# Modulation sums as column-tiled matmuls, and indexer scores in head pairs between the steps of the keys' projection

## What is computed

```python
mod = jax.nn.silu(c) @ ada_w + ada_b            # c: 1 x 1024, ada_w: 1024 x 6144
sh1, sc1, g1, sh2, sc2, g2 = jnp.split(mod, 6, axis=-1)
h = rms_norm(x, norm1_g) * (1.0 + sc1[:, None, :]) + sh1[:, None, :]
proj = h @ w_in                                 # 1024 x 2888
rq, rk, rv, rg, aq, ak, av, iq, ik, iw = jnp.split(proj, ...)
# indexer, for each block of 128 queries
rel = jnp.einsum('bqhe,bse->bqhs', qib, k_idx)  # 8 heads of 64
score = jnp.einsum('bqhs,bqh->bqs', jax.nn.relu(rel), wb)
score = jnp.where(causal, score, -jnp.inf)
_, sel = lax.top_k(score, 128)
# retention, attention over sel, then
x = x + g1 * (mix @ w_o)
h2 = rms_norm(x, norm2_g) * (1.0 + sc2) + sh2
y = moe(h2, ...)                                # 32 experts, the top 4 of each token
return rms_norm(x + g2 * y, final_g)
```

## Time and profile before

| | us |
|---|---|
| median of 3 runs | 1601.48 |
| lowest, highest | 1601.24, 1601.77 |
| the profiled execution, its own time | 1605.01 |
| its span, first to last instruction | 1603.2 |
| PE busy in the span | 1489.5 (93%) |
| DVE busy | 1329.3 (83%) |
| ACT busy | 1085.5 (68%) |
| POOL busy | 422.0 (26%) |

### The profile page before, as it was taken

How to read it: one execution, slowest core, us unless ns; L and a number is a source line. 1 busy time by engine, 2 the same in 40 slices (tenths; PEclk the granted TensorE clock), 3 DMA queues, 4 the chain that set the end, 5 groups by cost and what they waited for, 6 DMA issues and landing times.

```text
span 1603.2 us, 20619 instructions
## 1 busy us (share of the span) xinstructions
PE 1489.5 (93%) x6872; PEld 1185.7 (74%) x6872; DVE 1329.3 (83%) x1153; ACT 1085.5 (68%) x1126; POOL 422.0 (26%) x341
## 2 busy tenths in 40 slices
PE   3999996896799999999999999999999999999993
PEld 3667963455588888888888888888888888888872
DVE  4689957366599999998999999998999999998992
ACT  3554325333677777788877777788877777788881
POOL 1113510101113322233223322233223423233221
PEclk8899987996899999999999999999999999999996
DMA  9745510225499999999999999999999999999974
GB/s 348 219 156 184 184 54 14 60 79 202 177 365 372 364 364 373 374 370 382 360 372 371 370 365 372 370 375 379 357 378 370 376 348 370 382 379 368 362 272 132
DMA packets 95983, 483.70 MB, mean 302 GB/s; under 512 B 23416, under 2 KB 32752, under 8 KB 43632
## 3 DMA queue, kind: packets, MB, share of 16 engines
q1 hardware_dynamic: 83200, 450.47, 72.2%
q0 software_dynamic: 12752, 32.84, 8.6%
HBM read 469.09 MB, written 23.61 MB: 307 GB/s over the span
## 4 chain that ended last, share of the span: by engine, by line
PE 83%; DVE 9%; ACT 3%; DMA 3%; issue 1%; SPq 0%; POOLq 0%; DVEq 0%; POOL 0%; ACTq 0%
PE bank L1364 15%; PE bank L1363 15%; PE bank L1365 15%; PE bank L1385 7%; PE bank L1387 7%; PE bank L1386 7%; PE bank L1246 3%; PE bank L1344 2%; PE bank L1356 2%; PE bank L1336 2%; DVE w_lo L1474 2%; DMA ring<-in_ada_w 1%; PE bank L1067 1%; PE bank L1068 1%; PE bank L1069 1%
## 5 line engine op out<-in xcount | busy, mean ns | idle before, releaser
L1513 DVE TENSOR_TENSOR e_lo<-ring,e_hi 128x2048 fp32r<-128x2048 f32 x384 | 868.4, 2289 | 93.9 <-ACT e_hi L742 93.4
L742 ACT ACTIVATE e_hi<-ring 128x2048 fp32r<-128x2048 f32 x384 | 728.5, 1914 | 235.8 <-PE bank L1365 234.6
L1363 PE MATMUL bank<-e_hi,x_hi 128*128 128x512 f32 x1024 | 405.9, 396 | 1.6 <-DVE e_lo L1513 1.6
L1364 PE MATMUL bank<-e_lo,x_hi 128*128 128x512 f32 x1024 | 402.5, 393 | 0.0
L1365 PE MATMUL bank<-e_hi,x_lo 128*128 128x512 f32 x1024 | 398.8, 389 | 0.0
L1363 PEld LDWEIGHTS bank<-e_hi,x_hi 128*128 128x128 f32 x1024 | 192.7, 188 | 48.4 <-DVE e_lo L1513 2.5
L1364 PEld LDWEIGHTS bank<-e_lo,x_hi 128*128 128x128 f32 x1024 | 193.1, 189 | 40.0
L1365 PEld LDWEIGHTS bank<-e_hi,x_lo 128*128 128x128 f32 x1024 | 192.8, 188 | 40.2
L1385 PE MATMUL bank<-e_hi,act_hi 128*128 128x512 f32 x512 | 208.5, 407 | 0.1
L1387 PE MATMUL bank<-e_hi,act_lo 128*128 128x512 f32 x512 | 201.9, 394 | 0.0
L1386 PE MATMUL bank<-e_lo,act_hi 128*128 128x512 f32 x512 | 201.1, 393 | 0.0
(11 more groups left out here) (247 smaller groups left out, 1800.4 us busy)
## 6 DMA issues: line engine op xcount, KB each, us to landing
ring<-in_w_gu SPq DMA_DIRECT2D x256, 1024.0 KB, 8.6
ring<-in_w_down SPq DMA_DIRECT2D x128, 1024.0 KB, 7.3
ring<-in_ada_w SPq DMA_DIRECT2D x24, 1024.0 KB, 7.3
ring<-in_w_in SPq DMA_DIRECT2D x9, 1024.0 KB, 5.9
ring<-in_w_o SPq DMA_DIRECT2D x4, 1024.0 KB, 7.6
ring<-in_w_in SPq DMA_DIRECT2D x10, 256.0 KB, 5.9
sum_rows<-xs POOLq DMA_DIRECT2D x5, 512.0 KB, 4.5
xs<-in_x SPq DMA_DIRECT2D x4, 512.0 KB, 4.9
```

The source lines that it names most:

```text
L742: return nc.scalar.activation(dst, src, ACT.Copy, scale=scale)
L1363: pe.matmul(bank[b][:], x_hi[:, c, :], hi, start=False, stop=False)
L1364: pe.matmul(bank[b][:], x_hi[:, c, :], lo, start=False, stop=False)
L1513: tt(e_lo[c % PARTS][:], raw(period.raw_slot(c)), e_hi[:, c % PARTS, :].bitcast(F32), ALU.subtract).then_inc(lo_ready, 1)
```

## The change

The partial sums on ACT, DVE and POOL are gone. A piece of `ada_w` now stays in its slot, and PE multiplies it as it is: `mod_rows` issues four float32 matmuls for it, each with 32 equal columns of silu(c) as weights and 512 columns of the piece as the moving part. The four write the partition groups 0, 32, 64 and 96 of one bank, and eight pieces add up there. The bank is copied to `mrow` (by DVE for A, by ACT for the two halves of B, `rows_out_of_bank`), turned by four transposes (for A in the opening, for B in `rest_turned`), and `modA` and `modB` are read out of the turned rows; the gate rows g1 and g2 are added to their bias on 64 partitions (`gate_rows`) and stored by four DMAs.

The B pieces are now in the order of the two halves of their columns, and each is multiplied by PE just ahead of the half of `w_in` that follows it in `SEQUENCE` (`rest_rows`): three ahead of half 6, one, two, one and two ahead of halves 8, 10, 12 and 14, one and two ahead of the two parts of rg, two and one ahead of the two parts of rv, one behind rv. PE frees their slots.

The scores have a count and four banks (3 to 6) of their own. They are issued in pairs of heads, and behind each of the first eight pairs stands one step (three matmuls) of half 6. In the opening, the low parts of halves 0 and 1 stand behind `a1` on DVE. All four `sigmoid_rg` stand ahead of the eight takes of rv on ACT.

```diff
+            def mod_rows(b, n, k, used):
+                have(n)
+                for g in range(4):
+                    mm = pe.matmul(b[32 * g:32 * g + 32, :], sc_c[:, k:k + 1].broadcast_to((P, 32)),
+                                   slot(n)[:, 512 * g:512 * g + 512], start=(k == 0), stop=(k == KD - 1))
+                mm.then_inc(used, 1)
+            def rest_rows(low, high):
+                for i, n in enumerate(LOAD_B):
+                    if low < n < high:
+                        if i == KD:
+                            pe.wait_ge(mrow_ready, 2)
+                        mod_rows(bank[7], n, i % KD, rest_used)
+            def rest_turned(half):
+                j = (A_M0, A_M1)[half]
+                pe.wait_ge(mrow_ready, 2 + half)
+                free(j)
+                for q in range(4):
+                    mm = pe.transpose(abank(j)[:, q * P:(q + 1) * P], mrow[:, half, q * P:(q + 1) * P], ident[:])
+                mm.then_inc(act_full, 1)
+            pe.wait_ge(act_taken, A_VEC + 1)
+            pe.wait_ge(silu_ready, 1)
+            for k in range(KD // 2):
+                mod_rows(bank[0], LOAD_A[k], k, ada_used)
             pe.wait_ge(xn_ready, T)
             for k in range(KD):
                 if k == KD - 1:
-                    pe.wait_ge(act_taken, A_VEC + 1)
-                    pe.wait_ge(ada_used, KD)
-                    for m in range(16):
-                        mm = pe.matmul(bank[0][:, m:m + 1], acc[:, m * P:(m + 1) * P], ones[:, 0:1], start=True,
-                                       stop=True)
+                    for kk in range(KD // 2, KD):
+                        mod_rows(bank[0], LOAD_A[kk], kk, ada_used)
+                    pe.wait_ge(mrow_ready, 1)
+                    for q in range(4):
+                        mm = pe.transpose(bank[0][:, q * P:(q + 1) * P], mrow[:, 0, q * P:(q + 1) * P], ident[:])
                     mm.then_inc(mod_full, 1)
...
-                free(j)
-                pe.matmul(abank(j)[:, 0:(t + 1) * P], iqT[lo:lo + HD, h // 2, t * P:(t + 1) * P],
-                          ikT[lo:lo + HD, 0:(t + 1) * P], start=True, stop=True).then_inc(act_full, 1)
-            by_feature(A_AK, 6)
+                if n >= 4:
+                    pe.wait_ge(score_taken, n - 3)
+                pe.matmul(bank[3 + n % 4][:, 0:(t + 1) * P], iqT[lo:lo + HD, h // 2, t * P:(t + 1) * P],
+                          ikT[lo:lo + HD, 0:(t + 1) * P], start=True, stop=True).then_inc(score_full, 1)
+                if n % 2 == 1 and n // 2 < KD:
+                    by_feature(A_AK, 6, P, [n // 2])
...
-            for m in range(16):
-                mm = pe.matmul(bank[7][:, m:m + 1], acc[:, 1024 + m * P:1024 + (m + 1) * P], ones[:, 0:1],
-                               start=True, stop=True)
-            mm.then_inc(mod_full, 1)
-            for n, at in enumerate((0, 512, 3072, 3584)):
-                j = D_GROW + n
-                dfree(j)
-                pe.matmul(dbank(j)[0:1, :], ones[:, 0:1], acc[:, at:at + 512], start=True,
-                          stop=True).then_inc(dve_full, 1)
+            rest_rows(LOAD_W[-1], len(SEQUENCE))
```

On DVE:

```diff
-            for k in range(KD):
-                modulate(LOAD_A[k], 0, k, ada_used)
-                v.wait_ge(ada_used, k + 1)
-            w_lo_part(0)
-            w_lo_part(1)
+            v.wait_ge(ada_used, KD)
+            nc.vector.tensor_copy(mrow[:, 0, :], bank[0][:]).then_inc(mrow_ready, 1)
...
             v.wait_ge(affine_ready, 1)
+            w_lo_part(0)
             for k in range(KD):
+                if k == 2:
+                    w_lo_part(1)
```

On ACT:

```diff
+            rows_out_of_bank(0)
             for m in range(2):
                 take(A_RK + m, rkT[:, m, :], HD ** -0.5)
                 w_hi_part(18 + m)
+            turned_rows(0)
             for h in range(20, W_HALVES):
                 w_hi_part(h)
-            rest_scale(LOAD_W[-1], len(SEQUENCE))
             a.wait_ge(rel_added, 3 * IH)
-            sigmoid_rg(0)
-            sigmoid_rg(1)
+            for t in range(T):
+                sigmoid_rg(t)
             for c in range(2):
                 for t in range(T):
                     take(A_RV + c * T + t, rv[:, t, 256 * c:256 * c + 256], 1.0, abank(A_RV + c * T + t)[:, 0:256])
-            sigmoid_rg(2)
-            sigmoid_rg(3)
+            rows_out_of_bank(1)
```

More of the change, by code:

```diff
@@ L64 @@
 A_IT = A_IQ + 4
[L65 to L66 removed]
+A_AK = A_IT + 1
 A_AV = A_AK + 1
@@ L761, in _ @@
             copy(vecT[:], abank(j)[:, 0:72]).then_inc(act_taken, 1)
-            def rest_scale(low, high):
-                for n in B_POOL:
-                    k, r = n // 2, LOAD_B[n]
-                    if low < r < high:
-                        a.wait_ge(landed[r % SLOTS], 16 * (r // SLOTS + 1))
-                        copy(slot(r), slot(r), sc_c[:, k:k + 1]).then_inc(rest_scaled, 1)
             def w_hi_part(h):
@@ L835, in _, with rows_out_of_bank, turned_rows @@
                 w_hi_part(16 + m)
+            def rows_out_of_bank(half):
+                a.wait_ge(rest_used, KD * (half + 1))
+                copy(mrow[:, half, :], bank[7][:]).then_inc(mrow_ready, 1)
+            def turned_rows(half):
+                j = (A_M0, A_M1)[half]
+                src = abank(j).rearrange("p (j g r) -> p g j r", j=4, r=32)[:, 2 - 2 * half:4 - 2 * half, :, 0]
+                take(j, modB[:, 8 * half:8 * half + 8].rearrange("p (g j) -> p g j", g=2), 1.0, src)
+            rows_out_of_bank(0)
             for m in range(2):
@@ L1069, in exact, with by_feature @@
                 return pe.matmul(o, left_lo, right_hi, start=False, stop=last)
-            def by_feature(j, h, width=P):
+            def by_feature(j, h, width=P, steps=range(KD)):
+                if h % 2 == 0 and h > 0 and 0 in steps:
+                    rest_rows(LOAD_W[h // 2 - 1], LOAD_W[h // 2])
                 pe.wait_ge(w_lo_ready, h + 1)
@@ L1075, in by_feature @@
                 wh, wl = split_half(w_hi, h), split_half(w_lo, h)
-                for k in range(KD):
+                for k in steps:
                     if h == 0:
@@ L1114, in _ @@
                 by_feature(A_RK + m, 14 + m)
+            rest_turned(0)
             def by_token(o, h, t):
@@ L1164, in _ @@
                 elif h == 1:
-                    pe.wait_ge(affine_ready, 2)
+                    rest_turned(1)
                 pe.wait_ge(dve_taken, D_RS + h * T + T)
@@ L1448, in _ @@
             v.wait_ge(csig_ready, 1)
-            done(tt(sc_c[:], cs[:], csig[:], ALU.mult))
+            tt(sc_c[:], cs[:], csig[:], ALU.mult).then_inc(silu_ready, 1)
             v.wait_ge(rms_root, 1)
             nc.vector.reciprocal(ri[:, 0:T], rt[:, 0:T]).then_inc(rms_inv, 1)
-            def modulate(n, at, k, used):
-                v.wait_ge(landed[n % SLOTS], 16 * (n // SLOTS + 1))
-                o = acc[:, at:at + 2048]
-                if k == 0:
-                    ins = ts(o, slot(n), sc_c[:, k:k + 1], None, ALU.mult)
-                else:
-                    ins = stt(out=o, in0=slot(n), scalar=sc_c[:, k:k + 1], in1=o, op0=ALU.mult, op1=ALU.add)
-                ins.then_inc(used, 1)
-            def rest_sum(low, high):
-                for k in range(KD):
-                    if low < LOAD_B[2 * k] < high and 2 * k not in B_POOL:
-                        modulate(LOAD_B[2 * k], 0, k, rest_used[0])
-                        v.wait_ge(rest_used[0], k + 1)
             def w_lo_part(h):
-                if h % 2 == 0 and h > 0:
-                    rest_sum(LOAD_W[h // 2 - 1], LOAD_W[h // 2])
                 v.wait_ge(w_hi_ready, h + 1)
```

100 lines of the change are left out of this document (50 added, 50 removed).

## The result

The changed kernel takes **1613.44 us** (median of 4 runs, 1610.58 to 1616.37), the one before 1601.36 in runs on the same chip: ratio 1.007, 95% interval 1.0051 to 1.0088. It is slower by 12 us, where 4.7 was forecast. The direction and the mechanism that decides hold; the sum is too small.

What follows compares the result with a forecast made beforehand. PE was taken to bound the first part except the scores, which belong to DVE. The terms -7.8 - 2.8 + 5.6 + 7.6 + 2.1 = +4.7 us gave 1606.2 us from 1601.5, range 1597 to 1619.

Steps and rivals of the forecast that it cites:

- The stall that decides: In rv, PE fills three banks, then stands 13.9 us while ACT's sigmoids 2 and 3 wait for DVE's `rgs`.
- opening, halves 0 to 5: From the start through halves 0 to 5: 7.8 us gained, h starting at 34.2, halves ending at 72.6 instead of 80.4.
- scores and half 6: Scores with half 6 between pairs: PE sets the pace, 19.2 us instead of 22.0, 2.8 us gained.
- half 7 to R: From half 7 to the end of rg: 5.6 us lost, PE's nine pieces outweighing the pauses that go.
- R: The end of rg, at 180.3 us in the kernel before.
- R to the second matmuls: From the end of rg to the second retention matmuls (L1170): 48.9 us against 41.3, 7.6 us lost.
- behind them: From L1170 on: 2.1 us lost, L1170 taking 4.10 instead of 2.50 at the low clock, next L1159 0.5 more.
- The stall was there: Against the rival that PE runs through rv without a stall: 13.9 + 1.8 us less, 1590.5 us, chance 0.12.
- Two groups at a time: Rival on PE's pieces: only two column groups run together, 1.73 us a piece, 1618 to 1626 us, chance 0.13.
- The cold opening: Rival: clock stays low in the opening, pieces 5 to 8 at 1.73, a1 at 40.2, 1613 us, chance 0.10.
- its own case: Whole kernel: the four terms and the clock sum to +4.7 us, 1606.2 us, chance 0.63.

Runs made afterwards that it cites:

- second trace of the changed kernel: The changed kernel run again without any edit, 6 runs: 1613.37 us (1609.99 to 1615.39), ratio 1.0073.
- The experiment with the vector's copy first: Changed kernel with ACT's copy of vecT put ahead of its four copies of x: 1615.08 us, ratio 1.0073.

## Why the prediction was right in kind and short in size

**The step that failed is the size of the sum.** Up to the second retention matmuls it had +2.6 us; the trace has +8.6. The stall that decides was there as forecast. What the sum took over unchanged from the kernel before (the landing of the first weight piece, the price of a step in a row of its like) or took at the high clock did not hold. Each of its four terms was short, and all on the same side:

| term | forecast | measured | short by |
|---|---|---|---|
| opening, halves 0 to 5 | -7.8 | -5.6 | 2.2 |
| scores and half 6 | -2.8 | -1.3 | 1.5 |
| half 7 to R | +5.6 | +6.8 | 1.2 |
| R to the second matmuls | +7.6 | +8.8 | 1.2 |
| behind them | +2.1 | +3.3 by the medians | 1.2 |

The measured terms are differences of two single traces. In the second trace of the changed kernel they are -4.3, -1.3, +6.8 and +7.9, together +9.0: the two in the middle repeat, the first and the fourth move by some 1 us, so no more than that can be said of how short each was.

- **Opening, 2.2 short.** In the first trace the first weight piece decides, as the sum had it, and not `a1`. But it was taken to land at 32.86, as before, and ACT's high part starts at 34.62 (the last A piece too comes later: its rows start at 32.10, where 30.5 was assumed). Hence h at 35.73 instead of 34.2. The chain of waits of the changed kernel shows the load (start us, us, what):

```profile
22.97 0.39 SPq L444
23.40 5.08 SPq L445
28.52 6.08 DMA ring<-in_w_in
34.62 1.06 ACT w_hi L735
```

  The piece comes in three transfers. They are issued from 22.97, when PE has used its third A piece; before, with DVE freeing the pieces, from 20.39. The last one goes out at 28.52 instead of 26.98 and lands some 6 us later in both. The experiment with the vector's copy first issues them from 21.45, but the second issue then takes 6.52 us instead of 5.08, the last transfer goes out at 28.43, and the high part starts at 35.01. What lengthens the issue isn't shown; the 16 engines are full in both (share 1.02 from 17.9 to 28.0). DVE's last low part of h ends at 46.2 instead of 44.6; 0.4 more is PE's for its last four steps of half 0, which ends at 47.34, and 0.2 the five halves of 5.50.

  That `a1` doesn't decide is in part luck of this trace. `a1` was forecast at 33.6 and is done at 35.1. Of the eight traces with this opening, h waits for it in six, by 0.2 to 1.0 us; halves 0 to 5 end at 75.5 to 76.7 in the seven others.
- **Scores, right bound, short price.** PE sets the pace, as forecast. A step of three matmuls between two pairs takes 0.90 (79.76 - 78.86), where 5.45 / 8 = 0.68 was taken: 8 x 0.22 = 1.8 us, where the sum had 0.2 for all hand-overs of the stretch. The row the forecast went by (logits followed by transposes without a pause) has none of the first-matmul cost that 0.50 shows here beside 0.39. The trace of before has it, in the first matmul of half 6 behind the scores:

```profile
97.06 0.50 PE L1067 MATMUL bank<-h_hi,w_hi 128*128 128x512 f32 x1
```

  The Trainium skill ("TensorEngine Tiling (Array Packing)", Key Properties) has the rule that a change of tiling mode drains the engine; the trace agrees, with 0.2 us for the two changes of a step (0.11 behind the pair, 0.09 ahead of the next).
- **Half 7 to R.** A piece alone between other matmuls costs 1.0, each of two together 0.93, not 0.88: 8.7 us for the nine, where the sum had 7.9. The wait for the copy of bank 7 was 1.1 (1.4 forecast). The rest of the 1.2 was not taken apart.
- **R to the second matmuls, the term that decided.** Nearly exact: the first `rgs` at R + 22.7 (R + 22.6), PE's restart at R + 24.3, the pause 13.6 (13.9). Short is above all the group of rv behind the pause, at the low clock: 5.4 us (204.42 to 209.84) against 4.6, which was read from a shorter pause. It takes 4.8 us in the second trace of the changed kernel.
- **Clock behind it.** The second matmuls take 4.31 against 2.50, 1.8 of the 2.1. They are slow in all nine traces with the new modulation (3.92 to 4.63) and fast in all three with the old one (2.50). But before had a slow group of its own (237.94, 4.10), and from the start of these matmuls to the end of the span the changed trace is even shorter, 1378.3 against 1381.6. The traces of the experiments lie between 1377.2 and 1383.9 with the new modulation, at 1377.7 and 1380.2 with the old one. So a loss behind that point is not seen in the traces, and what of the 12 us lies there can't be placed by them; the 3.3 of the table is what is left of 12.0 (1613.44 less the 1601.48 that the forecast started from) behind the 8.6.

**The rivals.** The stall was there; taking it away (1595.17) shows that it is the whole loss and more. Two groups at a time: a further piece would read 1.73, and reads 0.87. The cold opening: pieces 5 and 6 take 1.92 together, not 3.5, and the transposes 3.28. Its tail end is real all the same: in five of the eight traces with this opening the last piece, behind a wait for its load, takes 1.90 to 1.94 us, and in six the four transposes of the rows take 1.1, some 1.3 us in all, which the sum lacks. The Trainium skill's rule ("TensorE: Matmul & The Clock Gate", Part 4), by which transposes don't count as activity for the clock, changed nothing here: behind 5.83 us of pieces all 28 ran at the high one, 0.12 us each. The forecast range held the result, since these rivals had widened it to 1619, not because the errors were sized: its own case was put at 1602 to 1611, and the 1613 of the cold opening is near the result by chance, since that rival had nothing gained in the opening, where the trace gains 5.6.

**A version that beats both** is the changed kernel with sigmoids 2 and 3 behind the takes: 0.9952 and 0.9958 of before in two sets of runs, 18 us under the changed kernel. Of its parts, neither alone shows in the time: pairs with the old modulation 1.0006 [0.9992, 1.0021], the new modulation without pairs 0.9992 [0.998, 1.0004]. The new modulation takes the sums off DVE; only then does PE's time in the scores count.

## What to carry to other kernels

When an instruction that waits for a third engine is moved ahead of those that empty PE's banks, count the banks and the way to what it waits for: PE runs that many groups and stands for the rest. Two sigmoids cost 18 us here, and the pause of PE could be worked out to 0.3 us from the trace of before alone. Saving on an engine pays only where that engine sets the pace behind the saving, so parts of a change are to be timed together and apart. And terms copied from the old trace (a landing, a matmul's price in a row of its like) erred to the same side, since the change frees the loads' buffers later and breaks up the rows: such errors add up. A term read from one trace is worth no more than that trace: the opening alone moved by up to 1.9 us between executions of the same code.

## What the runs showed of the hardware that was not expected

- Four column groups of 32 run fully side by side: 0.87 us for four float32 matmuls of 512 columns that would take 3.47 in a row (4.0 times as fast) in a run of pieces, 0.93 each for two between full matmuls and 1.0 for one (3.7 and 3.5 times).
- A step of three full matmuls between row-tiled pairs costs 0.90 us, not 0.68: the first of the three reads 0.50 instead of 0.39, and the last is followed by 0.32 to the next pair instead of 0.23.
- The same program's time differs by some 6 us from execution to execution, and the longer ones mostly have the lower mean granted clock: the changed kernel 1610 to 1611 us at 0.964 and 1615 to 1616 at 0.961, the kernel before 1598.4 at 0.961 and 1606.7 at 0.957. A trace against a trace is then uncertain by that much in the span. The start of the second retention matmuls is closer (230.19 and 230.58 in two traces of the changed kernel), but in part by chance: the opening of the second was 1.3 us longer and its last stretch 0.9 shorter.
- Whether the clock is still high after a wait of some 1.6 us differs from execution to execution: the last A piece took 1.06 us behind a wait of 1.56, and 1.90 behind one of 1.54.
- The last A piece arrives only at 32 to 33 us whether PE takes the first at 17.9 or at 15.6: from 17.9 to 28 us the 16 DMA engines are full in both traces (share 1.02, 423 and 424 GB/s).
